# FFN gate and up products with the weight tile as the standing operand and the 256 positions as the moving one

## The reference, cut to what matters

```python
D_FF = 256 * math.ceil(8 * D_MODEL / (3 * 256))      # 5632

def swiglu(h, w_g, w_u, w_d):
    return (jax.nn.silu(h @ w_g) * (h @ w_u)) @ w_d

        x = x + g2 * swiglu(modulate(rms_norm(x, norm2_w[i]), sh2, sc2),
                            w_ffn_gate[i], w_ffn_up[i], w_ffn_down[i])
```

## Time and profile before

| | |
|---|---|
| median of 3 runs | 2629.26 us (2627.51 to 2629.39) |
| the profiled execution, its own time | 2628.21 us |
| its span, first to last instruction | 2626.4 us |
| TensorE matmul busy | 2598.3 us, 99% of the span, 11874 records |
| TensorE weight load busy | 2140.8 us, 82% |
| VectorE busy | 1829.6 us, 70% |
| ScalarE busy | 1258.4 us, 48% |
| moved by DMA | 591.11 MB, mean 225 GB/s |
| FFN stage, first to last chunk | about 1888 to 2621 us |

### The profile page before, as it was taken

One profiled execution on the slowest core, in us unless ns is written; L12 is line 12 of the kernel. 1 busy time (PEld: TensorE's weight loads), 2 busy tenths in 40 slices (PEclk: granted clock), 3 DMA queues, 4 the chain that ended last, 5 costly groups with the idle time before them and its releaser, 6 DMA issues.

```text
span 2626.4 us, 30081 instructions
## 1 busy us (share of the span) xinstructions
PE 2598.3 (99%) x11874; PEld 2140.8 (82%) x11874; DVE 1829.6 (70%) x2209; ACT 1258.4 (48%) x1561; POOL 33.0 (1%) x35
## 2 busy tenths in 40 slices
PE   8999999999999999999999999999899999999999
PEld 7888878788887888888888878888788888888887
DVE  5887778898776877566666656667656666655557
ACT  5455543545554567544555544444544444444443
POOL 0000000000000000010000000000000000000000
PEclk9999999999999999999999999999999999999999
DMA  8865567586557867777766668777467777656554
GB/s 302 261 203 190 180 224 256 194 273 207 185 184 265 257 209 249 258 259 252 227 218 218 210 231 258 256 241 242 159 220 237 239 238 237 226 190 207 192 191 154
DMA packets 161596, 591.11 MB, mean 225 GB/s; under 512 B 17872, under 2 KB 18032, under 8 KB 160048
## 3 DMA queue, kind: packets, MB, share of 16 engines
q1 hardware_dynamic: 157696, 570.49, 66.2%
q0 software_dynamic: 2416, 11.93, 1.2%
q10 hardware_dynamic: 1344, 6.77, 0.6%
HBM read 587.01 MB, written 2.11 MB: 224 GB/s over the span
## 4 chain that ended last, share of the span: by engine, by line
PE 97%; DVE 2%; DMA 0%; ACT 0%; issue 0%; POOL 0%; SPq 0%; DVEq 0%; ACTq 0%
PE ps L708 30%; PE ps L710 30%; PE ps L709 30%; PE ps L724 1%; DVE w_lo L1085 1%; PE ps L770 1%; PE ps L950 1%; PE ps L866 1%; PE ps L934 1%; DMA raw<-weights 0%; PE ps L786 0%; PE ps L796 0%; PE ps L805 0%; PE ps L943 0%; PE ps L795 0%; PE ps L980 0%
## 5 line engine op out<-in xcount | busy, mean ns | idle before, releaser
L1085 DVE TENSOR_TENSOR w_lo<-raw,w_hi 128x1024 fp32r<-128x1024 f32 x888 | 1085.8, 1225 | 744.1 <-ACT w_hi L388 742.6
L388 ACT ACTIVATE w_hi<-raw 128x1024 fp32r<-128x1024 f32 x888 | 943.6, 1063 | 1327.1 <-PE ps L710 1232.2
L708 PE MATMUL ps<-w_hi,act_hi 128*128 128x512 f32 x3136 | 1243.5, 397 | 3.8 <-DVE w_lo L1085 2.6
L710 PE MATMUL ps<-w_hi,act_lo 128*128 128x512 f32 x3136 | 1223.4, 390 | 0.0
L709 PE MATMUL ps<-w_lo,act_hi 128*128 128x512 f32 x3136 | 1221.8, 390 | 0.0
L708 PEld LDWEIGHTS ps<-w_hi,act_hi 128*128 128x128 f32 x3136 | 589.6, 188 | 128.8 <-issue 9.3
L710 PEld LDWEIGHTS ps<-w_hi,act_lo 128*128 128x128 f32 x3136 | 589.2, 188 | 125.1
L709 PEld LDWEIGHTS ps<-w_lo,act_hi 128*128 128x128 f32 x3136 | 590.1, 188 | 120.8 <-issue 2.9
L1103 DVE SCALAR_TENSOR_TENSOR raw<-raw,c_row 128x1024 f32<-128x1024 f32 x192 | 234.1, 1219 | 0.1
L708 PE MATMUL ps<-w_hi,br_hi 128*128 128x512 f32 x416 | 162.6, 391 | 0.0
L709 PE MATMUL ps<-w_lo,br_hi 128*128 128x512 f32 x416 | 161.9, 389 | 0.0
(11 more groups left out here) (198 smaller groups left out, 1031.0 us busy)
## 6 DMA issues: line engine op xcount, KB each, us to landing
raw<-weights SPq DMA_DIRECT2D x888, 512.0 KB, 4.2
raw<-mods SPq DMA_DIRECT2D x192, 512.0 KB, 4.5
flat<-ln_gb POOLq DMA_DIRECT2D x4, 1024.0 KB, 8.5
x<-x_in SPq DMA_DIRECT2D x4, 512.0 KB, 10.0
flat<-conv_pw POOLq DMA_DIRECT2D x8, 256.0 KB, 4.9
shared<-na_rows POOLq DMA_DIRECT2D x2, 1024.0 KB, 9.1
flat<-ctx_in ACTq DMA_DIRECT2D x1, 2048.0 KB, 9.6
flat<-g_rows POOLq DMA_DIRECT2D x2, 1024.0 KB, 8.3
```

What stands on the lines that cost most here:

```text
L388: nc.scalar.activation(w_hi[:, n % SPLIT, :], raw[:, e % RAW, :], ACT.Copy).then_inc(hi_ready, 1)
L708: nc.tensor.matmul(acc, xh, wh, start=first, stop=False)
L710: mm = nc.tensor.matmul(acc, xl, wh, start=False, stop=last)
L1085: nc.vector.tensor_tensor(w_lo[:, j, :], raw_n, w_hi[:, j, :].bitcast(F32), ALU.subtract).then_inc(lo_ready, 1)
```

## The change

In ten of the eleven blocks (f = 1 to 10) the two operands of the gate and up products change places. The new function `chunk_across` takes a 128 x 128 tile of the weights as the standing operand and all 256 positions of `act_hi` or `act_lo` as the moving one. A chunk of these products holds eight K tiles by 128 columns in place of two K tiles by 512 columns (`put_across` lays the stream out so on the host; a chunk's size and the order of loads are as before). It is 24 matmuls of 256 columns, where it was 12 of 512. Two chunks make 128 hidden columns, in a quarter of the two banks. The products, and with them `kvc`, now have the hidden columns on the partitions, which is how the down product wants them: from block 1 on nothing is turned, and `hidden_hi` and `hidden_lo` read `kvc` instead of PSUM. Block 0 is made and turned as before. The down product is unchanged.

```diff
--- before.py
+++ after.py
@@ -669,9 +669,13 @@
             def silus():
                 nc.scalar.activation(gtmp[:, :, :], pair(2), ACT.Silu).then_inc(silu_done, 1)
 
-            def hidden_hi(f, hi, b=4):
-                act.wait_ge(hid_turned, f + 1)
-                nc.scalar.activation(hi, quarters(b), ACT.Copy).then_inc(hid_hi, 1)
+            def hidden_hi(f, hi):
+                if f:
+                    act.wait_ge(hid_ready, f + 1)
+                    nc.scalar.activation(hi.rearrange("p (a b) t -> p a (b t)", a=2), kvc[:, :, 0:COLS], ACT.Copy).then_inc(hid_hi, 1)
+                else:
+                    act.wait_ge(hid_turned, 1)
+                    nc.scalar.activation(hi, quarters(4), ACT.Copy).then_inc(hid_hi, 1)
 
             for f in range(FF):
                 for s in range(16 if f == 0 else 24):
@@ -691,7 +695,7 @@
                         if f:
                             hidden_hi(f - 1, br_hi[:, :, :])
                     if f == FF - 1 and s == 18:
-                        hidden_hi(f, act_hi[:, 0:4, :], 2)
+                        hidden_hi(f, act_hi[:, 0:4, :])
             for n in range(CHUNKS - 4, CHUNKS):
                 split(n)
 
@@ -1025,9 +1029,22 @@
             for r in range(4):
                 turn_h2(r)
 
-            def turn_hidden(f, b=4):
-                pe.wait_ge(hid_ready, f + 1)
-                turn_cols(b, lambda t, j: kvc[:, t, j * P:(j + 1) * P], hid_turned)
+            def turn_hidden():
+                pe.wait_ge(hid_ready, 1)
+                turn_cols(4, lambda t, j: kvc[:, t, j * P:(j + 1) * P], hid_turned)
+
+            def chunk_across(n, j, half, b):
+
+                pe.wait_ge(lo_ready, n + 1)
+                w = (w_hi[:, n % SPLIT, :], w_lo[:, n % SPLIT, :])
+                o = bank(b + j // 2, (j % 2) * S, (j % 2 + 1) * S)
+                for u in range(8):
+                    wh, wl = (v[:, u * P:(u + 1) * P] for v in w)
+                    k = 8 * half + u
+                    nc.tensor.matmul(o, wh, act_hi[:, k, :], start=k == 0, stop=False)
+                    nc.tensor.matmul(o, wl, act_hi[:, k, :], start=False, stop=False)
+                    mm = nc.tensor.matmul(o, wh, act_lo[:, k, :], start=False, stop=k == KT - 1)
+                mm.then_inc(chunk_used, 1)
 
             def down(q, s, f):
                 n = s // 2
@@ -1053,7 +1070,10 @@
                     if s < 16:
                         if f == 0 and s < 8:
                             pe.wait_ge(turn_lo, TURN_H2 + s + 1)
-                        chunk(q, of_group(s % 8, 2 if s < 8 else 0))
+                        if f:
+                            chunk_across(q, s % 8 // 2, s % 2, 2 if s < 8 else 0)
+                        else:
+                            chunk(q, of_group(s % 8, 2 if s < 8 else 0))
                     else:
                         down(q, s - 16, f - 1)
                     if f == 0 and s < 4:
@@ -1062,14 +1082,10 @@
                         pe.wait_ge(g_cols, 2)
                         pe.wait_ge(acc_done, 4 * (f - 1))
                         nc.tensor.transpose(bank(5, 256, 384)[0:KT, :], mod_x[:, 5 * KT:6 * KT], ident).then_inc(g_turned, 1)
-                    if f and s == 7:
-                        if f == 8:
-                            pe.wait_ge(g_copied, 2)
-                        if f >= 2:
-                            pe.wait_ge(acc_done, 4 * (f - 1))
-                        turn_hidden(f - 1)
-                    if f == FF - 1 and s == 17:
-                        turn_hidden(f, 2)
+                    if f == 1 and s == 7:
+                        turn_hidden()
+                    if f == 8 and s == 7:
+                        pe.wait_ge(g_copied, 2)
             for s in range(8):
                 down(CHUNKS - 8 + s, s, FF - 1)
 
@@ -1565,9 +1581,11 @@
                 dve.wait_ge(silu_done, f + 1)
                 nc.vector.tensor_tensor(kvc[:, :, 0:COLS], gtmp[:, :, :], pair(0), ALU.mult).then_inc(hid_ready, 1)
 
-            def hidden_lo(f, hi, lo, b=4):
+            def hidden_lo(f, hi, lo):
                 dve.wait_ge(hid_hi, f + 1)
-                rest_of(lo, quarters(b), hi).then_inc(hid_lo, 1)
+                if f:
+                    lo, hi = (v.rearrange("p (a b) t -> p a (b t)", a=2) for v in (lo, hi))
+                rest_of(lo, kvc[:, :, 0:COLS] if f else quarters(4), hi).then_inc(hid_lo, 1)
 
             for f in range(FF):
                 for s in range(16 if f == 0 else 24):
@@ -1578,7 +1596,7 @@
                     if f and s == 7:
                         hidden_lo(f - 1, br_hi[:, :, :], br_lo[:, :, :])
                     if f == FF - 1 and s == 18:
-                        hidden_lo(f, act_hi[:, 0:4, :], act_lo[:, 0:4, :], 2)
+                        hidden_lo(f, act_hi[:, 0:4, :], act_lo[:, 0:4, :])
                     if s == 15:
                         dve.wait_ge(chunk_used, q + 1)
                         hidden(f)
@@ -1672,6 +1690,15 @@
             stream[at // 2, :, at % 2, :] = w[k * P:(k + 1) * P, col * COLS:(col + 1) * COLS]
             at += 1
 
+    def put_across(w, col):
+
+        nonlocal at
+        for j in range(4):
+            cols = w[:, col * COLS + j * P:col * COLS + (j + 1) * P].reshape(2, 8, P, P)
+            for half in range(2):
+                stream[at // 2] = cols[half].transpose(1, 0, 2).reshape(P, 2, COLS)
+                at += 2
+
     for layer in range(DEPTH):
         for g in W_IN_ORDER:
             put_group(a["w_in"][layer], g)
@@ -1696,8 +1723,11 @@
     w_gate, w_up, w_down = (a[f"w_ffn_{n}_2"][0] for n in ("gate", "up", "down"))
     for f in range(FF + 1):
         if f < FF:
-            put_group(w_gate, f)
-            put_group(w_up, f)
+            for w in (w_gate, w_up):
+                if f:
+                    put_across(w, f)
+                else:
+                    put_group(w, f)
         if f:
             for g in range(D // COLS):
                 put_group(w_down, g, range(4 * (f - 1), 4 * f))
```

## The result

The changed kernel takes 2646.56 us (median of 4 runs, 2645.42 to 2648.03) beside 2629.32 us for the kernel before on the same chip: a ratio of 1.0067, 95% interval 1.0055 to 1.0079. It is slower by 17.2 us. The forecast was 2646.7 us. That the two agree to 0.1 us is luck: the four executions alone spread over 2.6 us. The profiled execution took 2645.42 us, its span is 2643.6 us.

A forecast was written before the change was run, and what follows sets the result against it. TensorE's matmuls were taken to bound the kernel: 2628.2 us, plus 25.6 for added matmuls, minus 8.2 for turns, gives 2645.6 us, so a median of 2646.7 us; range 2613 to 2664 us.

The forecast's parts named there:

- The bound: In the FFN stage TensorE waits for others only 0.7 us, so every microsecond on TensorE counts in full.
- Turns: Transposes of the hidden block on TensorE: nine leave blocks 2 to 10 at s = 7, saving 8.2 us.
- the tenth: The turn in block 10 at s = 17 goes too, but VectorE has no pause there: 0 us.
- Added matmuls: Gate and up chunks of blocks 1 to 10: 24 matmuls at 120.0 ns, +0.16 us for each of 160 chunks, +25.6 us.
- The weight load fits: An fp32r weight load needs about 110 ns of its own, under the 113 to 120 ns between matmuls.
- the stalled start: Where TensorE had stood waiting, the load at 2603.44 was followed by the next at 2603.55: about 110 ns a load.
- Copies at no cost: ScalarE's hidden-block copy takes about 1.06 us from SBUF, 1.02 from PSUM; idle time and VectorE's slack cover the moved work.
- The sum: 2628.2 + 25.6 - 8.2 = 2645.6 us for the profiled execution; median 2646.7 us, slower by 0.7%.
- by the matmul: In gate and up products the 13.3 ns beyond the columns belong to each matmul: 120.0 ns at 256 columns; chance 0.50.
- The columns rival: In gate and up products the 13.3 ns go with the columns, chunks stay at 2.72 us: 2621.1 us; chance 0.28.

The follow-up runs named there:

- nine out: The kernel before with the nine turns at step 7 of blocks 2 to 10 left out, copies reading the unturned hidden block: 2620.87 us, ratio 0.9968.
- Halves: The kernel before, turns and operands in place, each gate and up matmul of blocks 1 to 10 cut into two of 256 columns: 2654.42 us, ratio 1.0097.
- quarters: The changed kernel with each matmul of the exchanged products cut into two of 128 positions, 48 a chunk: 3042.52 us, ratio 1.1573.
- Half a load: The kernel before, each gate and up matmul of blocks 1 to 10 made as two of 512 columns with 64 positions standing, not 128: 3077.32 us, ratio 1.1707.

## Why the prediction was right

- **The bound.** TensorE's chain, nothing waited for: confirmed by the waits after, and by the runs' times, which follow from the pitch within 3 us.
- **Turns, -8.2 us.** Measured -8.4 us in the stage (nine out), and 0 for the tenth, as argued from VectorE's rows.
- **Added matmuls, +25.6 us.** Halves, which are this term alone, measured +25.2 us between medians and +25.3 us in the stage. The pitch is 120.0 ns, the value taken.
- **The weight load fits.** It needs 112 ns (quarters); 110 had been read from the stalled start.
- **Copies at no cost.** Confirmed; ScalarE's idle behind them is used up.
- **The sum.** 25.6 - 8.2 = 17.4 us; measured 17.2 us between medians and 17.3 us in the stage. The two terms measured one by one in the stage give 25.3 - 8.4 = 16.9 us, so they add up within 0.4 us, and no closer.
- **A range that was worked out wrong.** For a settled extra of 10.5 to 17 ns the prediction gives 2640 to 2654 us. 3840 matmuls make 3.84 us of each nanosecond, so it should have been 2636 to 2661 us. Nothing else hangs on it.

One argument was weaker than its result. I chose "by the matmul" because five starts after a disturbance took 230 ns each for the same columns. Half a load shows that 230 ns can also be a lasting pitch, and bfloat16 shows an extra that grows with the length under the same kind of timeline. What shows the choice right for fp32r is the row of three lengths, 256, 384 and 512, which the trace of before didn't have. The columns rival deserved its chance, and the right choice between the two owes something to luck.

By the formula of the Trainium skill, "TensorE: Matmul & The Clock Gate", section "Back-to-back issue gap", 256 columns would take 109 ns, an estimate; that section gives the formula for an isolated matmul and says that it leaves out the weight load. No run in fp32r or in strided bfloat16 came to it: the shortest pitch for 256 columns was 113.3 ns. The same page's section "LDWEIGHTS (loading the stationary operand)" has P / 1.2 ns, which is 107 ns for a load of 128 columns; the quarters' 112 ns agree within 5 ns.

No version here that makes the reference's products from the whole fp32r values beats the kernel before. The one with bfloat16 and 256 columns takes 7.2 us less (ratio 0.9973), but it leaves out the lower half of every value. The nine turns can bring 8.4 us at most, 0.84 us a block counted over the ten that the change touches, and 192 more matmuls a block cost 192 x 13.3 ns = 2.56 us.

## What to carry to other kernels

When a change swaps the standing and the moving operand, count matmuls, not only columns: in fp32r every matmul took 13.3 ns more than its columns at 256, 384 and 512 columns, and at 128 columns the load's 112 ns was the bound. Find the fixed part by measuring the settled pitch at two or three lengths: one length alone can't tell a fixed part from a slower rate. Then test it by cutting one matmul in two where nothing else moves. Eight transposes of 109 ns are cheap beside twice as many matmuls.

## What the runs showed of the hardware that was not expected

- The pitch of fp32r matmuls, each with its own weight load, was 226.7, 173.3 and 120.0 ns at 512, 384 and 256 columns at the 2.4 GHz level, and 112 ns at 128, where the weight load bounds. Four loads of 64 rows each, on the two halves of the rows in turn (L795 of the kernel before), took 55 ns each, so the 112 ns are not the pace of instructions.
- bfloat16 operands read at every second element gave 225.0 ns at 512 and 113.3 ns at 256 columns. Whether it is the type or the step of two that leaves 11.7 and 6.7 ns was not tried.
- Standing operands of 64 columns shorten the load's record from 0.19 to 0.13 us and don't shorten the pitch: it was 230 ns at 512 columns. Where the 13.3 ns arise inside TensorE, and whether they belong to the matmul or to its load, stays open.
